# Later layers in two parts of 128 and 384 tokens, the second interleaved with retrieval in blocks of 32 tokens x 4 picks

## What is computed

```python
mod = silu(c) @ ada_w + ada_b              # 6 x 2048: shift1, scale1, gate1, shift2, scale2, gate2
h = rms_norm(x, g0) * (1 + scale1) + shift1
proj = h @ w_in                            # q, k, v (12 heads), glu, gates
attn = dilated_window_attention(...) @ w_attn_o
conv = silu(layer_norm(depthwise_conv31(glu))) @ w_conv_o
y = (sigmoid(g_attn) * attn + sigmoid(g_conv) * conv) @ w_out
x = x + gate1 * rms_norm(y, g1)
h = rms_norm(x, g2) * (1 + scale2) + shift2
q = h @ w_q                                # 8 heads x 2 halves
s1, s2 = q . sub_keys                      # 128 scores each; top 16 of each, then top 16 of the sums
pre = h . peer_down[expert]                # 128 picks a token: 8 heads x 16
act = gelu(pre) * softmax(top)
y = sum(act * peer_up[expert])
x = x + gate2 * rms_norm(y, g3)
```

## Time and profile before

| | |
|---|---|
| median of 3 runs | 4541.33 us (4539.33 to 4544.47) |
| span of the profiled execution | 4541.7 us |
| TensorE busy | 3503.3 us, 77% |
| VectorE busy | 2220.1 us, 49% |
| ScalarE busy | 618.2 us, 14% |
| GpSimd busy | 1707.2 us, 38% |
| moved by DMA | 1343.76 MB, of it gathers 1073.81 MB |
| mean granted TensorE clock | 0.953 |

### The profile page before, as it was taken

One profiled execution on the slowest core, in us unless ns is written; L12 is line 12 of the kernel. 1 busy time (PEld: TensorE's weight loads), 2 busy tenths in 40 slices (PEclk: granted clock), 3 DMA queues, 4 the chain that ended last, 5 costly groups with the idle time before them and its releaser, 6 DMA issues.

```text
span 4541.7 us, 32957 instructions
## 1 busy us (share of the span) xinstructions
PE 3503.3 (77%) x10853; PEld 2020.6 (44%) x10853; DVE 2220.1 (49%) x2895; ACT 618.2 (14%) x1007; POOL 1707.2 (38%) x1208
## 2 busy tenths in 40 slices
PE   3777869697999987947777777777777777777777
PEld 2665768674667766812222232222322222322223
DVE  7335264445445014375665445664446654444442
ACT  2211212130112232200010010100101001110000
POOL 1456263522224332343333333333333333333332
PEclk9888989898999998979999999999999999999999
DMA  7421212146666332199999999999999999999997
GB/s 289 167 74 65 75 65 93 62 138 227 217 207 222 113 129 102 63 421 421 422 422 422 422 416 421 422 421 422 405 422 422 422 419 422 402 422 422 422 422 292
DMA packets 259545, 1343.76 MB, mean 296 GB/s; under 512 B 23360, under 2 KB 23552, under 8 KB 125184
## 3 DMA queue, kind: packets, MB, share of 16 engines
q0 software_dynamic: 147456, 1073.81, 57.0%
q1 hardware_dynamic: 104128, 243.29, 15.7%
q10 hardware_dynamic: 7872, 25.54, 1.5%
HBM read 1330.93 MB, written 11.62 MB: 296 GB/s over the span
## 4 chain that ended last, share of the span: by engine, by line
PE 43%; DMA 42%; DVE 6%; POOL 4%; issue 3%; ACT 1%; POOLq 0%; ACTq 0%; SPq 0%; DVEq 0%
PE psum L557 43%; DMA front<-in_up,back 38%; POOL w_low L479 4%; DMA back<-in_ada_w 2%; DMA front<-in_down,back 1%; DVE back L1217 1%; DVE front L1489 1%; DVE back L1362 0%; ACT back L1134 0%; DVE back L1390 0%; DVE back L1304 0%; DVE x_low L1403 0%; DVE back L1396 0%; DVE back L1397 0%; DVE back L1391 0%
## 5 line engine op out<-in xcount | busy, mean ns | idle before, releaser
L557 PE MATMUL psum<-front,back 128*128 128x512 f32 x4096 | 1907.1, 611 | 693.5 <-DMA front<-in_up,back 618.2
L1489 DVE CUSTOM_DVE_ANT_0 front<-front,psum 128x2048 f32<-128x2048 f32 x512 | 1165.3, 2287 | 1115.0 <-DMA front<-in_down,back 1094.2
L557 PEld LDWEIGHTS psum<-front,back 128*128 128x128 f32 x4096 | 751.7, 193 | 1848.3 <-issue 1617.8
L479 POOL TENSOR_TENSOR w_low<-front,w_high 128x2048 fp32r<-128x2048 f32 x116 | 678.2, 5848 | 1130.5 <-ACT w_high L869 667.5
L509 POOL DMA_INDIRECT front<-in_up,back x512 | 485.5, 948 | 1399.8 <-PE psum L557 1339.5
L557 PE MATMUL psum<-x_high,w_high 128*128 128x512 f32 x1408 | 560.6, 398 | 150.1 <-POOL w_low L479 121.1
L509 POOL DMA_INDIRECT front<-in_down,back x512 | 487.1, 951 | 208.8 <-issue 157.4
L557 PE MATMUL psum<-x_low,w_high 128*128 128x512 f32 x1408 | 556.6, 395 | 0.0
L557 PE MATMUL psum<-x_high,w_low 128*128 128x512 f32 x1408 | 555.6, 395 | 0.0
L557 PEld LDWEIGHTS psum<-x_high,w_high 128*128 128x128 f32 x1408 | 270.2, 192 | 211.5 <-POOL w_low L479 122.8
L1129 ACT ACTIVATE back<-back 128x16 f32<-128x16 f32 x32 | 7.0, 218 | 2284.4 <-DVE back L1489 2284.4
(11 more groups left out here) (165 smaller groups left out, 1676.5 us busy)
## 6 DMA issues: line engine op xcount, KB each, us to landing
front<-in_w_in SPq DMA_DIRECT2D x84, 1024.0 KB, 5.1
back<-in_ada_w SPq DMA_DIRECT2D x128, 512.0 KB, 4.1
back<-in_ada_w SPq DMA_DIRECT2D x32, 1024.0 KB, 7.4
front<-in_w_out SPq DMA_DIRECT2D x16, 1024.0 KB, 5.1
front<-in_w_q SPq DMA_DIRECT2D x16, 1024.0 KB, 5.0
back<-in_x ACTq DMA_DIRECT2D x8, 1024.0 KB, 10.9
front<-in_w_conv_o SPq DMA_DIRECT2D x8, 1024.0 KB, 7.0
front<-in_down,back POOLq DMA_INDIRECT x512, 16.5
```

The costliest lines, as they stand in the source:

```text
L479: nc.gpsimd.tensor_tensor(wl[s], ring[s], wh[s % 2].bitcast(fp32), ALU.subtract).then_inc(w_low_done, 1)
L557: return nc.tensor.matmul(o, a, b, start=start, stop=stop)
L1489: V.tensor_tensor_reduce(row, row, h2p, 1.0, 0.0, ALU.mult, ALU.add, pre[:, s:s + 1]).then_inc(dots_done, 1)
```

## The change

What the new kernel does:

- The front is the same (its loops are written out). After it, high and low parts of h are added to `hT` (fp32), and all later products are plain fp32, with no splitting on ScalarE and GpSimd.
- The later layers are one function `tail(c)`, called for tokens 0 to 127 and then for tokens 128 to 511, on each engine. Both read all the weights, through a ring of three 1 MB buffers. Channels stay on partitions; the norms sum squares over partitions with products with a matrix of ones.
- The conditioning products (64 of 128 x 2048) are loaded by GpSimd's queue through four buffers and taken by VectorE in `tail(0)`.
- Retrieval runs in 16 groups of 32 tokens, 32 blocks each. A block is 4 picks for each of 32 tokens; the sixteen block index and gate pieces are written by `route` and `gates`. h2 of the group is spread to four partition quarters by TensorE (`h2_quarter`) and copied to SBUF (`h2r`, one buffer). Weighted rows: a stationary tile of 128 x 32, and four products that each write 32 partitions of one PSUM bank. Up rows run 22 blocks behind in the queue and 24 on TensorE.
- In `tail(1)` each engine calls `retrieve` after each chunk of weights, up to the block that `PACE` names: 128 blocks in 83 chunks.
- Buffers: three down and three up rows for the first 160 blocks, then five and five.

The core of the diff (`retrieve`, `passed` and `tail` have the same form on TensorE, ScalarE and VectorE):

```diff
-UNITS = TT * PH
-NB = 8
-UB = 4
+TAIL = ((0, P), (P, S - P))
+GROUPS = TT * 4
+BLOCKS = GROUPS * 32
+LAG = 24
+UP_LAG = 22
+WIDE = 160
+END = BLOCKS + 64
...
+def block_pace():
+    at, out = 0, []
+    for i in range(tail_chunks(1)):
+        if 64 <= i < 67:
+            at += (3, 3, 2)[i - 64]
+        else:
+            at += 1 + i % 2
+        out.append(at)
+    assert at == 128, at
+    return out
+D_KB, U_KB = (64, 72, 80, 0, 8), (88, 96, 104, 16, 169)
+D_SLOT = slot_table(3, len(D_KB))
+U_SLOT = slot_table(3, len(U_KB))
...
 # GpSimd
-            with pool.Fori(1, 21) as G:
+            for G in range(1, 13):
                 for s in range(4):
                     low(G, s)
-            for k in range(12):
-                mix_low(k)
...
+            pool.wait_ge(h_joined, 4)
+            for n in range(4 * KT):
+                if n >= 4:
+                    pool.wait_ge(ada2_used, n - 3)
+                j, i = n // KT, n % KT
+                nc.gpsimd.dma_start(ada_ring[n % 4], ada_w[i * P:(i + 1) * P, (2 + j) * D:(3 + j) * D]).then_inc(ada2_in[n % 4], 16)
...
+            pool.wait_ge(ada2_used, 4 * KT)
+            for i in range(BLOCKS + UP_LAG):
+                if i < BLOCKS:
+                    s, _, prev = D_SLOT[i]
+                    if i % 128 < 32 and i % 8 == 0:
+                        pool.wait_ge(routed, 4 * (i // 128) + i % 128 // 8 + 1)
+                    if prev is not None:
+                        pool.wait_ge(dots_done, prev + 1)
+                    if i == WIDE:
+                        pool.wait_ge(g_done, DONE[1, "sc", 3] + 4)
+                    gather(down, d_row[s], i, d_in[s])
+                b = i - UP_LAG
+                if b >= 0:
+                    s, _, prev = U_SLOT[b]
+                    if prev is not None:
+                        pool.wait_ge(u_used, prev + 1)
...
+                    gather(up, u_row[s], b, u_in[s])
 # TensorE
+            def h2_quarter(J, i):
+                if i or J:
+                    pe.wait_ge(h2r_ready, 4 * J + i)
...
+                for k in range(4 * i, 4 * i + 4):
+                    for s in range(4):
+                        ins = mm(ps[32 * s:32 * s + 32, 7, k % 4 * P:(k % 4 + 1) * P],
+                                 hT[:, k, 32 * J:32 * J + 32], ident, True, True)
+                ins.then_inc(h2r_done, 1)
+            def weighted_rows(b):
+                s, fills, _ = U_SLOT[b]
+                J = b // 32
+                pe.wait_ge(diag_ready, b + 1)
+                pe.wait_ge(u_in[s], 16 * (fills + 1))
+                if b % 32 == 0 and J >= 2:
+                    pe.wait_ge(z_read, J - 1)
+                for c in range(4):
+                    ins = mm(ps[32 * c:32 * c + 32, 4 + J % 2, :], diag[:, b % 32, :],
+                             u_row[s][:, c * NT:(c + 1) * NT], b % 32 == 0, b % 32 == 31)
+                ins.then_inc(u_used, 1)
+                def group(chunks, per, src, place, free, base, between=None):
+                    for s in range(chunks):
+                        r = tring[chunk_in()]
+                        for m in range(4):
+                            if s == 0 and free is not None:
+                                pe.wait_ge(free, base + m + 1)
+                            for k in range(per):
+                                ins = mm(ps[:, m, 0:n], r[:, k, m * P:(m + 1) * P], src[:, place(per * s + k), tok],
+                                         s == 0 and k == 0, s == chunks - 1 and k == per - 1)
...
+                        chunk_out(c)
 # ScalarE
+            def h2_quarters(J):
+                for i in range(4):
+                    act.wait_ge(h2r_done, 4 * J + i + 1)
+                    if J and i == 0:
+                        act.wait_ge(dots_done, 32 * J)
+                    A(h2r[:, i * NT:(i + 1) * NT], ps[:, 7, :], ACT.Copy).then_inc(h2r_ready, 1)
+                A(diag[:, b % 32, :], same[:, 0:32], ACT.Copy, scale=actv[:, n % 2, b % 16:b % 16 + 1]).then_inc(diag_ready, 1)
 # VectorE
+            def dot(b):
+                s, fills, _ = D_SLOT[b]
+                if b % 32 == 0:
+                    dve.wait_ge(h2r_ready, 4 * (b // 32 + 1))
+                dve.wait_ge(d_in[s], 16 * (fills + 1))
+                V.tensor_tensor_reduce(d_row[s], d_row[s], h2r, 1.0, 0.0, ALU.mult, ALU.add,
+                                       pre[:, b // 16 % 2, b % 16:b % 16 + 1]).then_inc(dots_done, 1)
+                    if c == 0:
+                        condition(cg, 0, 10)
+                    passed(c, 9)
+                    for m in range(4):
+                        dve.wait_ge(act_took, ATOOK[c, "ga", cg] + m + 1)
+                        dve.wait_ge(g_done, DONE[c, "ao", cg] + m + 1)
...
+                for i in range(4):
+                    passed(c, 4)
+                    dve.wait_ge(act_took, ATOOK[c, "sc", i] + 4)
+                    route(c, i)
+                    if i:
+                        gates(c, i - 1)
+                gates(c, 3)
```

## The result

The changed kernel takes **4466.47 us** (median of 4 runs, 4462.66 to 4471.04) against 4542.74 us of the kernel before on the same chip: a ratio of 0.9827, 95% interval 0.9813 to 0.9841, 1.7% faster. I had forecast 4572 us, slower. Its profiled execution has a span of 4469.0 us.

What follows compares the result with a forecast made beforehand. It took TensorE to bound the kernel before 1927 us and gather bytes to bound retrieval. Parts ending at 1388 us, then 1143 and 2041, gave 4572 us; own range 4500 to 4640, with rivals 4440 to 4850.

Steps and rivals of the forecast that it cites:

- Stretch 1 and 2: Front, 912 us, then later layers for tokens 0 to 127, 476 us, mostly waiting for weight bytes; end at 1388 us.
- Stretch 3: Later layers for tokens 128 to 511 with 128 retrieval blocks in between, bound by TensorE: 1143 us.
- the price of a block: TensorE's four weighted-row products between chunks: half overlapped, 1.71 us a block, 178 us for 104 blocks.
- rival (b): All four quarter products run at once on TensorE: tokens 128 to 511 take 1040 us, total 4453; chance 0.18.
- The waits: TensorE's idle time during tokens 128 to 511: boundaries 20, normalisation chain 55, scores' turns 14, late rows 17; 106 us.
- The turns of the scores: TensorE's waits at the scores for tokens 128 to 511: 14 us.
- The boundaries: TensorE's waits at three group boundaries during tokens 128 to 511: 20 us.
- Stretch 4: Rest of retrieval after the later layers, bound by bytes: 787 gathers, 1957 us, plus stops; 2041 us.
- the stop at 128: Last routing and two gate steps before dot 128, with only three down buffers filled: 30 us of nearly idle queues.
- Rival (c): Rings too short, POOL's single queue blocks: each of 12 boundaries costs 10 us more, total 4692; chance 0.12.
- Rival (d): No overlap: dots wait for TensorE's chunks during tokens 128 to 511; size and 0.12 chance within Rival (c)'s.
- (a): No overlap of the quarters on TensorE: 3.43 us a block, total 4833 us; chance 0.22.

Runs made afterwards that it cites:

- experiment 6: The changed kernel with 60 of 64 conditioning loads cut to 512 of 2048 columns, modulations computed from stale data: 4377.09 us.
- experiment 1: The changed kernel with all four weighted-row products writing the first 32 partitions in 30 of 32 blocks of a group: 4702.06 us.
- experiment 2: The changed kernel with the four weighted-row products writing two quarters, two in each, in 30 of 32 blocks of a group: 4520.04 us.
- experiment 3: The changed kernel with all 128 retrieval blocks run behind the last but one chunk instead of between the chunks: 4929.68 us.
- experiment 5: The changed kernel with seven down buffers in place of five from block 160 on: 4454.37 us.
- experiment 10: The changed kernel with six down and five up buffers from position 131, last routing of tokens 128 to 255 at 142, two h2 buffers from group 5: 4421.7 us.

## Why the prediction was wrong, step by step

The forecast had the kernel some 30 us slower than before; it is 76 us faster. So the direction was wrong too, by the steps that follow.

**The frame held.** Four stretches, TensorE the bound of the third and bytes that of the fourth, are what the trace shows, and of the marks that I had set, the first down gather came at 1358 (forecast near 1345) and at most boundaries the dots start 9.7 to 11.0 us apart, which leaves a stop of 7.4 to 8.7 (forecast about 9).

**Stretch 1 and 2: right, by two errors that cancel.** 1393 against 1388. TensorE begins the second column group at 991 us and not 1000, and the three groups take 80, 78 and 80 us and not 75 each. That bytes set them is borne out by experiment 6.

**Stretch 3, the step that failed: the price of a block.** The argument that "with records started in order only the second of one and the first of the next can overlap" set it at 1.71. It took 1.04: 107 us and not 178, 71 of the 120. Experiments 1 and 2 measure the rule that I should have had: 3.60, 1.91 and 1.07 us with one, two and four quarters. One visit to the quarters in the changed kernel, record by record:

```profile
1638.60 0.49 PE L559 MATMUL psum<-back,front 128*128 128x384 f32 x1
1639.02 0.64 PE L559 MATMUL psum<-front 128*32 128x512 f32 x4
1639.47 0.61 PE L559 MATMUL psum<-front 128*32 128x512 f32 x4
1640.01 0.59 PE L559 MATMUL psum<-back,front 128*128 128x384 f32 x1
1640.44 0.49 PE L559 MATMUL psum<-back,front 128*128 128x384 f32 x1
1640.76 0.49 PE L559 MATMUL psum<-back,front 128*128 128x384 f32 x1
```

Four records start together and the other four 0.45 us later. Records of one quarter never did (experiment 1: eight in 3.60 us), so the first four belong to four different products. My argument had assumed that the two records of a product run one behind the other before the next product starts; they don't. The Trainium skill's rule that I set aside ("TensorE: Matmul & The Clock Gate", Part 3: products in distinct 32-partition strips run at once, three in 1/2.38 of the time) is what the runs show, here 3.60 / 1.07 = 3.4 for four; rival (b) had 1040 for this stretch and 4453 in all.

**The waits: second step that failed.** 106 us forecast, 57 measured. TensorE in order of time in the normalisation chain, with idle time before each:

```profile
2136.99 2.85 PE L559 MATMUL psum<-back 128*128 128x384 f32 x8
...
2158.49 1.93 PE L559 MATMUL psum<-front 128*32 128x512 f32 x8 [3.68 <-DMA front<-in_up,back]
2171.00 1.94 PE L559 MATMUL psum<-front 128*32 128x512 f32 x8 [4.50 <-DMA front<-in_up,back]
...
2186.48 13.46 PE L559 MATMUL psum<-back 128*128 128x384 f32 x32 [2.48 <-ACT back L1144]
2214.71 3.57 PE L559 MATMUL psum<-front 128*128 128x384 f32 x5 [14.77 <-ACT front L1149]
```

The chain is 78 us long, as forecast (75), but TensorE is idle in it for 36 us only, against 55. And the 36 contain nearly all the waits in front of weighted rows (17.7 of 18.4 us, 4.3 of them for ScalarE), which I had priced as 17 of their own: outside the chain they are 0.7. The turns of the scores, 14 in the forecast, cost nothing: TensorE shows no idle time from 2214.71 to the end of the stretch. One stop of 6.3 us at 1934.16, in front of the output projection, was not in my sum; the profile puts it to "issue", so what ended it is not known. The boundaries took 13.8 of their 20. 19 + 16 + 14 + 6 less 6 are the 49. I had added up single stops, each priced as if nothing else ran; the waits overlap each other, and in experiments 1 and 2 they give way to work (32 and 39 us where the blocks cost 350 and 190). That is the part of the miss which experiment 2 has too. In the total the two failed steps weigh about the same: 52 us from the forecast to experiment 2 (4572 to 4520), which has nearly the forecast's price, and 54 from there to the changed kernel.

**Smaller terms.** 384-column work with scores and turns took 834 us (965.4 less the blocks, the spreading and the products of x2) against 823. Spreading took 19 against 30, the products of x2 4 to 5 against 6. So 1143 + 11 - 71 - 49 - 12 = 1022. The usual record starts 0.322 us after the last, as forecast (half of 0.645). Behind the 11 stand some 8 from 24 records that start mostly 0.64 us after the last, twice the usual and so at the lower level of the clock, behind idle stretches of TensorE, and some 6 from the record behind each visit to the quarters; the other work came out 3 under.

The Trainium skill's other rule, that a change of tiling mode drains TensorE ("TensorEngine Tiling (Array Packing)", Key Properties), I had priced at up to 30 us and left out of the sum. The visit shown above has such a cost. Its first record starts 0.42 us after the last full one, not 0.32; the next full one 0.52 us after the last four, where records of one quarter stand 0.43 apart (experiment 1); and the second full one again 0.43 later, not 0.32. That is about 0.1 us three times, 0.3 a visit, and it is the same to 0.01 us in nearly all of 64 visits: some 18 us in all, spread over the terms above. In experiment 3, where the chunks run without visits, full records 0.43 us apart occur three times in place of 59. So the trace agrees that a change costs time; by which mechanism, no run shows.

**Stretch 4: right size, wrong inside.** 2053 against 2041. I had the stop at 128 at 30; the dots stand 30.5 us apart there, but the bytes missing are 23. Boundaries I had as covered. Not seen: at positions 156 to 160 a routing, a boundary with h2's single buffer and the change from three buffers to five meet, and leave a hole of 15 to 18 us. Rival (c)'s mechanism, one POOL queue that alternates two kinds, is real; it decides only there and behind the routings, for 12 us (experiment 5) to 43 (experiment 10, which moves the stops too) and not for its 120. Rival (d) falls by experiment 3: 864 and 622 us alone are 1023 together.

**The chances.** I gave the case that came true 0.18, against (a) with 0.22. The trace had nothing for either, and the faster one had the Trainium skill's figure beside it. "The only price shown" is a price for full columns and says nothing of quarters; I should not have counted it as evidence for no overlap. What stays open: whether the 7 to 17 us of holes behind 2900 come from the routings alone; no run took the routings away.

## What to carry to other kernels

When a change splits a product over the array, ask first which partitions each part writes; that place alone made 236 us here, between a kernel slower than before and one that is faster. Work bound by TensorE and work bound by bytes can share their time if they are interleaved finely: 864 and 622 us became 1023, not 1486. And where several kinds of stop (a routing, a refilled single buffer, a ring that changes size) can coincide, place them apart or double the buffer: singly, behind ten buffers, they cost little here (17 us behind 2900 for five routings and nine boundaries), but together 15 to 18 at one place.

## What the runs showed of the hardware that I had not expected

**The clock falls when the work gets cheap, and it costs nothing here.** TensorE in order of time in retrieval alone, changed kernel:

```profile
3001.83 1.93 PE L559 MATMUL psum<-front 128*32 128x512 f32 x8 [3.15 <-DMA front<-in_up,back]
```

The eight records of a block, which took 1.07 us at a granted clock of 0.97, take 1.93 at one of 0.50 to 0.55, the lower of the two levels (1.2 GHz), after TensorE stood idle for 3 us of every 5. With one quarter (experiment 1) the block lasts 3.60, the idle time is about 1.4 of 5, and the windows show the upper level most of the time:

```profile
3900.00:4300.00 400.00, 295.56 (x1104) 80.48 (x1103) 184.33 (x171) 35.08 (x111) 201.60 (x156) 0.91 1.01 421
```

and the changed kernel:

```profile
3900.00:4300.00 400.00, 165.23 (x1092) 39.33 (x1092) 187.90 (x174) 34.04 (x108) 177.91 (x159) 0.55 1.01 421
```

Both move 421 GB/s. Only bytes count there, and the lower clock costs nothing.

**A gather that starts beside a dot product ends after it.** On POOL a gather takes 932 ns at best, as before, but up to 3046, and those of down have a mean of 1221 (951 before). In order of time in the changed kernel, a dot and two gathers, and then a gather of the kernel before, which starts while the dot at 2004.14 in the earlier trace rows still runs:

```profile
3000.68 2.28 DVE L1459 CUSTOM_DVE_ANT_0 front<-front,back 128x2048 f32<-128x2048 f32 x1
3001.87 1.91 POOL L530 DMA_INDIRECT front<-in_down,back  x1 [0.30 <-issue]
3009.15 0.94 POOL L530 DMA_INDIRECT front<-in_down,back  x1 [0.30 <-issue]
```

```profile
2005.73 0.94 POOL L509 DMA_INDIRECT front<-in_up,back  x1 [2.81 <-PE psum L557]
```

The gather at 3001.87 starts under the dot and ends some 0.8 us after it; the one at 3009.15 starts while no dot runs. In the whole changed kernel 229 gathers start while a dot runs; 217 of them take over 1.2 us, and these end 0.80 to 0.81 us after the dot does. Of the 795 others none takes over 1.2 us. In the kernel before, whose dot reads h2 from PSUM, 496 gathers start beside a dot and none takes over 1.2 us. So the sign that I had set, a dot slowed by POOL (over 2.5 us), did not come: the dot takes 2.292 us against 2.287, and it is the gather that waits. That it is h2 in SBUF which makes it wait is what the two kernels differ in there, but no run changes it alone. In retrieval POOL has time for it.
